# Output bias folded into the last combine, accumulator cleared by VectorE, and three items of the first expert pair kept outside the ring

## The reference

```python
gates = softmax(top_4(h @ w_router + b_router))
gu = h @ w_gu[e] + b_gu[e]                 # 1024 -> 2 x 1024
gate = minimum(gu[:, :1024], 7.0)
up = clip(gu[:, 1024:], -7.0, 7.0)
y_e = ((up + 1) * gate * sigmoid(1.702 * gate)) @ w_d[e] + b_d[e]
x = x + gt2 * sum_over_4(gates[e] * y_e)
y = rmsnorm(x, g_final)
```

## Time and profile before

| | |
|---|---|
| time, 3 runs | 1333.23, 1336.16, 1340.67 us; median 1336.16 |
| the profiled execution | 1335.32 us, its span 1333.7 us (1.6 us lie around the span) |
| mean granted TensorE clock | 0.972 of full speed |
| PE busy | 1216.4 us (91%) |
| DVE, ACT, POOL busy | 318.6, 174.3, 48.8 us |
| moved | 500.51 MB, mean 375 GB/s over the span |

### The profile page before, as it was taken

How to read it: one execution, slowest core, us unless ns; L and a number is a source line. 1 busy time by engine, 2 the same in 40 slices (tenths; PEclk the granted TensorE clock), 3 DMA queues, 4 the chain that set the end, 5 groups by cost and what they waited for, 6 DMA issues and landing times.

```text
span 1333.7 us, 15276 instructions
## 1 busy us (share of the span) xinstructions
PE 1216.4 (91%) x5982; PEld 609.9 (46%) x5982; DVE 318.6 (24%) x574; ACT 174.3 (13%) x343; POOL 48.8 (4%) x93
## 2 busy tenths in 40 slices
PE   5999998999999989898989989898989889898987
PEld 2788755688543424243242424243342424243343
DVE  2379865333212011102001110111021011102032
ACT  2132231100210200110020002001000200010012
POOL 0121231000000000000000000000000000000000
PEclk9899999999898999999999999999999999999989
DMA  9998998974499999999999999999999999999991
GB/s 352 330 357 291 381 334 335 393 296 138 190 400 414 370 415 411 413 408 417 414 419 414 421 415 421 414 420 416 417 420 413 421 411 420 415 420 416 404 409 44
DMA packets 105774, 500.51 MB, mean 375 GB/s; under 512 B 8601, under 2 KB 10759, under 8 KB 69984
## 3 DMA queue, kind: packets, MB, share of 16 engines
q1 hardware_dynamic: 98960, 478.38, 89.5%
q0 software_dynamic: 6496, 21.42, 4.6%
q10 hardware_dynamic: 272, 0.09, 0.0%
HBM read 496.48 MB, written 3.38 MB: 375 GB/s over the span
## 4 chain that ended last, share of the span: by engine, by line
PE 73%; DMA 22%; ACT 2%; DVE 1%; issue 1%; SPq 1%; DVEq 0%
PE ps L926 26%; DMA ring<-in_w_d 20%; PE ps L440 11%; PE ps L978 10%; PE ps L826 4%; PE ps L1055 4%; PE ps L876 3%; PE ps L374 3%; PE ps L803 2%; PE ps L758 2%; DMA ring<-in_w_ada 2%; PE ps L405 1%; PE ps L614 1%; ACT oT L1329 1%; PE ps L998 1%
## 5 line engine op out<-in xcount | busy, mean ns | idle before, releaser
L926 PE MATMUL ps<-ring,zone 128*64 128x512 f32 x2032 | 442.7, 592 | 2.8 <-issue 2.8
L978 PE MATMUL ps<-ring,oT 128*64 128x512 f32 x1024 | 246.5, 638 | 69.5 <-DMA ring<-in_w_d 69.5
L926 PEld LDWEIGHTS ps<-ring,zone 128*64 128x64 f32 x2032 | 147.7, 137 | 289.7 <-issue 287.2
L978 PEld LDWEIGHTS ps<-ring,oT 128*64 128x64 f32 x1024 | 77.5, 146 | 237.5 <-issue 156.6
L1877 DVE TENSOR_SCALAR zone<-ps 128x1024 f32<-128x1024 f32 x16 | 19.6, 1225 | 625.5 <-PE ps L926 625.4
L440 PE MATMUL ps<-hT,ring 128*128 128x264 f32 x640 | 152.5, 397 | 2.1 <-DVE hT L1466 1.8
L440 PEld LDWEIGHTS ps<-hT,ring 128*128 128x128 f32 x640 | 123.1, 195 | 29.6 <-issue 7.4
L1324 ACT ACTIVATE attn<-zone 128x1024 f32<-128x1024 f32 x16 | 16.9, 1057 | 502.9 <-DVE zone L1877 502.9
L826 PE MATMUL ps<-zone,dec_scores 128*64 128x512 f32 x256 | 59.3, 604 | 0.0
L1894 DVE TENSOR_TENSOR zone<-zone,ps 128x264 f32<-128x264 f32 x56 | 24.1, 430 | 145.5 <-PE ps L1055 145.5
L374 PE MATMUL ps<-ident,zone 128*128 128x128 f32 (+3 forms) x212 | 32.0, 277 | 16.5 <-DMA zone<-in_b_alpha 10.9
(11 more groups left out here) (367 smaller groups left out, 776.8 us busy)
## 6 DMA issues: line engine op xcount, KB each, us to landing
ring<-in_w_gu SPq DMA_DIRECT2D x127, 2048.0 KB, 17.6
ring<-in_w_d SPq DMA_DIRECT2D x62, 2048.0 KB, 15.6
ring<-in_w_ada SPq DMA_DIRECT2D x12, 2048.0 KB, 12.8
ring<-in_w_in SPq DMA_DIRECT2D x9, 2048.0 KB, 13.6
ring<-in_cache_k SPq DMA_DIRECT2D x32, 256.0 KB, 7.4
ring<-in_cache_k POOLq DMA_DIRECT2D x32, 256.0 KB, 6.6
ring<-in_cache_v SPq DMA_DIRECT2D x32, 256.0 KB, 9.7
ring<-in_cache_v POOLq DMA_DIRECT2D x32, 256.0 KB, 8.2
```

Of the source, the lines that this page charges most:

```text
L926: ins = pe.matmul(ps[64 * j:64 * j + CAP, c, :], xg[:, k, 2 * par + j, :], rows, start=False, stop=(k == KT - 1), skip_group_check=True)
L978: ins = pe.matmul(ps[64 * j:64 * j + CAP, 4 + c, :], hidT[:, k, j * CAP:(j + 1) * CAP], w[j][:, kk, c * 512:(c + 1) * 512], start=(k == 0) ...
```

## The change

- `SPARES = 3`: items 5, 6 and 7 of pair 0 get places outside the ring. Item 6 stays where it was. Item 7 goes to `hT` and the first 2048 columns of `zone` (2 loads, after the signal `x1_sums`). Item 5 goes to `oT`, `tok[:, 2, :]`, `rows_512` and 512 columns of `put` (4 loads, after the signal `mixed`), and to `attn` (1 load, after `pick_ready`).
- The numbers of all later items fall by 3, so that number 5, item 0 of pair 1, takes the slot of wo1 ahead of any use by PE. PE counts the three by a signal of their own, `spares_used`, on which DVE's first `swiglu` waits. PE waits once for all loads of the three (`spares_landed`), ahead of step s = 2 of the first `gate_up`. The stand-in increment of the landing semaphore is gone.
- `output_bias` is gone on PE and on DVE. DVE clears `acc` with a memset in the first quad, after it has copied the turned gates. `put` is cleared after the first `swiglu` instead of before. The product of `b_d` and gates becomes the first term of the sums of the `combine` in the last quad (`biased`). `down` of pair 0 waits for `gatesT`, and the counts of `added` and `summed` fall by 8.
- `second_half_landed` gives names of first-part signals that are used twice.

```diff
+SPARES = 3
-        spare = [[gate_hid[:, c * 512:(c + 1) * 512] for c in range(4)],
-                 [ye_tok[c // 2][:, (c % 2) * 512:(c % 2 + 1) * 512] for c in range(4)]]
+        spare = {6: [[(gate_hid, 0, 2 * FF)], [(ye_tok[0], 0, FF), (ye_tok[1], FF, FF)]],
+                 7: [[(hT_flat, 0, 2 * FF)], [(zone, 0, 2 * FF)]],
+                 5: [[(oT_flat, 0, FF), (tok[:, 2, :], FF, FF)],
+                     [(attn_flat, 0, FF), (rows_512, FF, 512), (put_512, FF + 512, 512)]]}
...
         def gate_up_done(n, first):
-            return n * 12 + (8 if first else 4)
+            return n * 12 + (8 if first else 4) - SPARES
...
             at_ = (i if edge else i - 4) if kind == "gu" else (8 + i if edge else 16 + i)
+            at_ -= 0 if kind == "gu" and edge and isinstance(n, int) and n == 0 else SPARES
...
-                    in_spare = cold and edge and s == 3
-                    if in_spare:
-                        pe.wait_ge(sig("spare_landed"), 48)
+                    in_spare = [cold and edge and 2 * s + j >= 8 - SPARES for j in range(2)]
+                    if cold and edge and s == (8 - SPARES) // 2:
+                        pe.wait_ge(sig("spares_landed"), 16 * sum(len(h) for i in range(8 - SPARES, 8) for h in spare[i]))
...
                                 if kk == 1 and c == 3:
-                                    ins.then_inc(sig("slots_used"), 1)
-                                if cold and edge and s == 0 and kk == 1 and c == 2 and j == 0:
-                                    ins.then_inc(landed[EXPERT_SLOTS[0]], 16)
+                                    ins.then_inc(sig("spares_used" if in_spare[j] else "slots_used"), 1)
...
-            def combine(q):
+            def combine(q, biased):
+                if biased:
+                    pe.wait_ge(sig("b_d"), 16)
+                    pe.wait_ge(sig("gatesT"), 1)
                 pe.wait_ge(sig("ye_ready"), q * 2 + 2)
...
+                    if biased:
+                        pe.matmul(ps[:, 6 + m % 2, 0:T], b_d_sb[:, m * P:(m + 1) * P], gatesT, start=True, stop=False)
                     for par in range(2):
                         ins = pe.matmul(ps[:, 6 + m % 2, 0:T], ye_tok[par][:, m * P:(m + 1) * P], putT[:, par, :],
-                                        start=(par == 0), stop=(par == 1))
+                                        start=(par == 0 and not biased), stop=(par == 1))
...
-                    if cold:
-                        output_bias()
...
+                if cold:
+                    pe.wait_ge(sig("gatesT"), 1)
                 down(q, 0, False, cold)
...
-                quad(q + (QUADS - 1), False, True, False)
+                quad(q + (QUADS - 1), False, True, False, biased=cold)
...
             def quad(q, qq, first, last, cold):
                 swiglu(q, 0, first)
+                if cold:
+                    chain(V.memset(put, 0.0))
...
                 if cold:
-                    output_bias()
+                    dve.wait_ge(sig("gates_turned"), 1)
+                    V.tensor_copy(gatesT, ps[0:NE, 4, 0:T]).then_inc(sig("gatesT"), 1)
+                    chain(V.memset(acc, 0.0))
...
+            def load_spare(i, kk, n):
+                home, c0, width = spare[i][kk][n]
+                k = 2 * (i // 2) + kk
+                sp.dma_start(home[:, 0:width], w_gu[0, i % 2, k * P:(k + 1) * P, c0:c0 + width])\
+                    .then_inc(sig("spares_landed"), 16)
...
+                    if phase_one and kind == "gu" and edge:
+                        if i == 2:
+                            sp.wait_ge(sig("gla_done"), 1)
+                            sp.wait_ge(sig("gla_stored"), 32)
+                            load_whole_spare(6)
+                        if i == 4:
+                            sp.wait_ge(sig("mixed"), 1)
+                            load_spare(5, 0, 0)
+                            load_spare(5, 0, 1)
+                            load_spare(5, 1, 1)
+                            load_spare(5, 1, 2)
+                        if i == 5:
+                            continue
+                        if i == 6:
+                            continue
+                        if i == 7:
+                            sp.wait_ge(sig("x1_sums"), 1)
+                            load_whole_spare(7)
+                            continue
+                    if phase_one and kind == "gu" and not edge and i == 1:
+                        sp.wait_ge(sig("pick_ready"), 1)
+                        load_spare(5, 1, 0)
```

More of the change, by code:

```diff
@@ L301, in gate_up_done @@
         def gate_up_done(n, first):
-            return n * 12 + (8 if first else 4)
+            return n * 12 + (8 if first else 4) - SPARES
         def down_done(n, last):
-            return n * 12 + (12 if last else 20)
+            return n * 12 + (12 if last else 20) - SPARES
         def expert_load(kind, i, n, edge):
             at_ = (i if edge else i - 4) if kind == "gu" else (8 + i if edge else 16 + i)
+            at_ -= 0 if kind == "gu" and edge and isinstance(n, int) and n == 0 else SPARES
             slot = EXPERT_SLOTS[at_ % SLOTS]
@@ L318, in page_of, with second_half_landed @@
             return (i, n) if item[0] == "K" else (4 * (i // 4) + n % 4, 2 * (i % 4) + n // 4)
+        def second_half_landed(item):
+            i = int(item[1:])
+            again = i >= 4 and item != "K7"
+            return sig(f"second_half_{item[0]}{i - 4 if again else i}"), 16 * (PAGES // 2) * (2 if again else 1)
         def load_pages(eng, item, half, done, slot_free):
@@ L608, in cached_values @@
                 arrived(pe, item)
-                pe.wait_ge(sig(f"second_half_{item}"), 16 * (PAGES // 2))
+                pe.wait_ge(*second_half_landed(item))
                 v = slot_ap(item)[:, 0:PAGES * WA].rearrange("p (j c) -> p j c", j=PAGES)
@@ L851, in turn_gates @@
                 ins.then_inc(sig("gates_turned"), 1)
[L853 to L862, removed]
             def gather(q, cold):
@@ L924, in gate_up @@
                             for j in range(2):
-                                rows = spare[kk][c] if w[j] is None else w[j][:, kk, c * 512:(c + 1) * 512]
+                                rows = spare_columns(2 * s + j, kk, c) if in_spare[j] else w[j][:, kk, c * 512:(c + 1) * 512]
                                 ins = pe.matmul(ps[64 * j:64 * j + CAP, c, :], xg[:, k, 2 * par + j, :], rows,
@@ L938, in turn_hidden @@
                         pe.wait_ge(sig("read"), q * 10 + (3 + 2 * par + g))
-                    if par == 1:
-                        pe.wait_ge(sig("added"), q * KT + (7 + g))
+                    if par == 1 and not cold:
+                        pe.wait_ge(sig("added"), q * KT + (g - 1))
                     for k in range(4):
@@ L1071, in quad @@
                     turn_hidden(q, 0, cold, first)
-                    combine(q - 1)
+                    combine(q - 1, biased)
                     gate_up(q, 1, False, False)
+                if cold:
+                    pe.wait_ge(sig("gatesT"), 1)
                 down(q, 0, False, cold)
-                turn_hidden(q, 1, cold, first and not cold)
+                turn_hidden(q, 1, cold, first)
                 turn_put(q)
@@ L1875, in swiglu @@
                 n = q * 2 + par
+                if isinstance(n, int) and n == 0:
+                    dve.wait_ge(sig("spares_used"), SPARES)
                 dve.wait_ge(sig("slots_used"), gate_up_done(n, first))
@@ L1992, in rounds_and_gates @@
                 dve.wait_ge(sig("gates"), 1)
[L1994 to L2001, removed]
             one_round(0)
@@ L2088, in _, with load_whole_spare @@
             dn = w_d[0].rearrange("e (k p) c -> e p k c", p=P)
[L2090 to L2095, removed]
+            def load_spare(i, kk, n):
[3 more added lines that the diff above has]
+                    .then_inc(sig("spares_landed"), 16)
+            def load_whole_spare(i):
+                for kk in range(2):
+                    for n in range(len(spare[i][kk])):
+                        load_spare(i, kk, n)
             def load_expert(kind, n, pair, edge, phase_one=False, rows=None):
@@ L2182, in second_half @@
             def second_half(item):
-                load_pages(pool, item, 1, sig(f"second_half_{item}"), freed[slot_before(item)])
+                load_pages(pool, item, 1, second_half_landed(item)[0], freed[slot_before(item)])
             arrived(pool, "ka")
```

32 lines of the change are left out of this document (17 added, 15 removed).

## The result

Slower: 1341.64 us against 1333.25 (medians of 20 runs each), a ratio of 1.0054 with a 95% interval of 1.0033 to 1.0075, or 7.2 us. The ratio is of the fast runs alone, which leaves out one run of the changed kernel (1353.38 us); the medians are of all. I had forecast 1.9 us less, and 1327 to 1339. The profiled execution has a span of 1344.3 us, 10.6 above the one of before.

A forecast was written before the change was run, and what follows sets the result against it. The expert part was taken as bound by bytes, with the DMA queue empty at times because the ring is full. -5.5 + 3.6 = -1.9 us took 1335.32 to 1333.4, or 1334.2 for a median; range 1327 to 1339.

The forecast's parts named there:

- the gain of 5.5 us: Second quad: old item 26 begins at 457.3 instead of 462.8, 5.5 us earlier, which includes the head's 1.9.
- Outside items: First lull: two more items fill empty time; queue full 362 to 387, empty until 396, 1.9 us left of 10.1.
- Rival A: Head: the head start is kept whole, -10.1 + 3.6 = -6.5 us, 1329.7; chance 0.10.
- D: First gate_up: the single wait for three outside items holds PE; clearly slower, +0.5% needs landing past 375; chance 0.06.
- Bias out of the first quad: First quad: without output_bias, down ends at 435.7 instead of 441.1 and the next gate_up begins at 448.3 instead of 453.7.
- A lead kept to the end: Loops after the second quad: the 5.5 us gain enters the final sum unchanged, with no term for loss.
- Bias in the last combine: Last quad: 16 bias records at 0.23 us each, say 3.6 us, all on PE's path, moving the end by 3.6.
- The upper bound, 5.4: Last combine: the bias costs at most 5.4 us, if its products ran as in output_bias.
- The sum: Whole kernel: -5.5 + 3.6 = -1.9 us, 1335.32 becomes 1333.4, 1334.2 for a median.
- Rival B: Last quad: the bias is hidden, the dip at 1248 being not the ring; -5.5 us, 1330.7; chance 0.13.
- C: Second quad: PE not early, gap at 458 stays, 1.9 won against 3.6 paid; +1.7 us, 1337.9; chance 0.09.
- first-byte figure: SP loads: first byte at some 0.6 us, in place of 1.9, would make the gain about 6.8 instead of 5.5.

The follow-up runs named there:

- e11: Changed kernel with only items 6 and 7 outside the ring, item 5 back in it, and the bias in the first quad; ratio to the kernel before 1.0006.
- e3: Changed kernel with b_d and the turned gates padded by zero rows to 128 for the bias products; ratio to the kernel before 1.0012.
- e2: Kernel before with the bias part alone: bias products in the last combine, acc cleared by memset, one item outside; ratio to the kernel before 1.0044.
- e4: Changed kernel with the bias products left out altogether, so the output lacks the share of b_d; ratio to the kernel before 0.9990.
- e5: Changed kernel with the eight 32-row bias products in each of the seven combines instead of the last alone; ratio to the kernel before 1.0353.
- e6: Changed kernel with bias products padded to 128 rows in each of the seven combines; ratio to the kernel before 1.0162.
- e1: Changed kernel with the bias put back in the first quad, ahead of down, three items still outside; ratio to the kernel before 0.9978.
- e7: Changed kernel with the bias in the first quad, between the two halves of the first down; ratio to the kernel before 0.9981.
- e12: Repeat measurement of the changed kernel with the bias put back in the first quad, three items outside; ratio to the kernel before 0.9989.
- e9: Changed kernel with products of no use, five ahead of the first half of each down and three ahead of the second; ratio to before 1.0087.
- e10: Changed kernel with bias in the first quad and products of no use, two ahead of each down's first half, one ahead of second; ratio to before 1.0047.

## Why the prediction was wrong

Two steps of the sum failed: the gain of 5.5 us, of which 2.8 were there at 520 in the traced execution and nothing at 600, and the 3.6 us for the bias in the last combine, which made that combine 6.4 longer and cost 6.1 in the lead.

**Outside items: right.** Issues at 303 to 305, 340 and 349, the queue full to 387 and empty to 397, step 2 of the first `gate_up` without a wait. Rival A fell as said, and e11 shows it from the other side. D did not happen. The memsets of VectorE took 1.82 and 0.70 us and delayed nothing.

**Bias out of the first quad: the place right, the size off.** I had `gate_up` of the second quad at 448.3; it began at 450.9. The second half of the first `down` started at 429.50 (I had 428.6) and took 8.8 us instead of 7.1, behind a wait of 4.49; the granted clock from 429 to 434 was 0.66:

```profile
417.93 7.09 PE L984 MATMUL ps<-ring,oT 128*64 128x512 f32 x32 [1.07 <-DMA ring<-in_w_d]
429.50 8.78 PE L984 MATMUL ps<-ring,oT 128*64 128x512 f32 x32 [4.49 <-DMA ring<-in_w_d]
...
450.89 27.64 PE L934 MATMUL ps<-ring,zone 128*64 128x512 f32 x128
481.03 8.78 PE L984 MATMUL ps<-ring,oT 128*64 128x512 f32 x32 [2.50 <-DMA ring<-in_w_d]
492.79 9.99 PE L984 MATMUL ps<-ring,oT 128*64 128x512 f32 x32 [2.98 <-DMA ring<-in_w_d]
```

So 2.8 us were won by 520 instead of 5.5. I had taken PE's work at its full clock and left out that the products behind a wait can go at half of it.

**A lead kept to the end: false.** My sum carries the 5.5 us from the second quad to the end unchanged; for what the loops between may lose it has no term, and I gave no reason. In the changed kernel all of the lead was lost by 590. Near 492 the second half took 10.0 us instead of 7.1 (the last row above), the next use that frees a slot came that much later, and the queue ran dry at 523; again 8.7 at 557 and the dip at 585. In that half the granted clock was 0.50 (the lower level, 1.2 GHz) from 493 to 498, and 1.00 again from 500 on:

```profile
493.00:496.00 3.00, 3.00 (x8) 0.90 (x8) 0.00 (x0) 0.00 (x0) 0.00 (x0) 0.50 1.01 421
500.00:503.00 3.00, 3.00 (x17) 1.07 (x14) 0.00 (x0) 0.16 (x1) 0.00 (x0) 1.00 1.01 421
```

The place of the bias makes it likely, but not certain. Of the executions without filling, those with the bias out of the first quad (the changed kernel, e2, e3, e4, e5, e6) had second halves of 10.0, 9.7, 8.6, 8.5, 10.1 and 7.1 us there, behind waits of 3.0, 4.3, 2.7, 2.6, 2.8 and 2.5; those with it in (before, e1, e7, e11, e12) 7.1, behind 1.8, 0.4, 0.2, 0.3 and 1.4. The first four lost 4.6, 3.7, 1.1 and 1.1 us from 520 to 600. e5 lost 9.4 and e6 3.4, with one biased combine in that stretch, which costs 6.1 and 3.3; so about 3.3 and nothing are left for the halves. Those with the bias in lost nothing. e4 is the changed kernel up to the last quad, so between 1.1 and 4.6 lies the chance of an execution, and what settles it is open. The times are the better measure: the ratio of e4 (1.3 us ahead of before) says that of the 5.5 us forecast some 4 were not there. e9, with PE kept busy, lost 0.4.

The same step is found far behind the first quad too, with the bias in:

```profile
1031.39 9.94 PE L997 MATMUL ps<-ring,oT 128*64 128x512 f32 x32 [3.14 <-DMA ring<-in_w_d]
1060.00:1064.00 4.00, 4.00 (x21) 1.30 (x18) 0.00 (x0) 0.00 (x0) 0.00 (x0) 1.00 0.52 129
```

These are a second half of e12 and the stretch 29 us on, where 2.5 us of its lead went. e2 had two more, of 10.05 and 10.06 us at 1042.8 and 1165.7, and lost 2.7 and 2.4 us behind them.

**Bias in the last combine: mis-sized.** "16 records: 3.7 us, say 3.6" should have been 6.4. That it would be wholly on the path was right (6.1 us by the lead). I priced a record by the mean of a combine in which all are of one height, and took from L861 that fewer rows are no quicker; neither row can show what a neighbour of another height costs. At one height it would have come out: 10.9 us in e3 against 7.36 are 3.5. The upper bound, 5.4, had the same hole.

**The sum.** With what was measured: -2.8 + 4.6 + 6.1 = +7.9 us, and +2.7 more in the profiled execution. Those 2.7 are open: all second halves of that stretch took 7.1. e1 and e12 are the same kernel, and their steps from 600 to 1240 are +0.6 and +3.9, of which 2.5 follow the one long half above; the rest seems to be chance of an execution. By the times of many runs the account is: 1.3 us won without the bias (e4), 8.5 us lost by the bias (the changed kernel against e4), in sum 7.2 slower, where I had 5.5 won and 3.6 lost; each of the two carries some 3 or 4 us of uncertainty. By the ratio the change costs 7.2 us.

Rival B was wrong: nothing of the bias was hidden at the end. C is nearest to the outcome, a lead that is not there when the bias has to be paid, but not by its own sign: the second quad's `gate_up` came at 450.9 and not later than 452, and the lead was lost afterwards.

By the first-byte figure of the Trainium skill (DMA: Bandwidth & Descriptors, Specifications) the second quad's `gate_up` would, by my estimate, have come 1.3 us ahead of my 448.3, and it was 2.6 behind. That does not test the figure by itself, for PE's slow half is in it. The slow start of the trace stands: issued at 395.26, the loads moved 207 GB/s from 395 to 399, so full rate counts from 397.0, 1.75 us behind the issue.

## What to carry to other kernels

In a loop that is bound by bytes through a ring, ask for each place whether PE's next use is what lets the next load go. If so, every microsecond of PE's is paid there, and the same work can be nearly free elsewhere, where PE waits for data: in e1 the 5.8 us of bias made the second quad's `gate_up` 1.1 us later than in the changed kernel, at the same lead at 400. The best of the versions tried leave the bias in the first quad and keep the outside items, at 0.998 and 0.999 (e1 and e12, one kernel) and 0.998 (e7).

Price a product with its neighbours: in this combine a few of another height among tall ones made all of them slower, and padding with zero rows was cheaper. And a wait of PE's can cost more than itself, by the slower products behind it, in one execution and not in the next: read more than one trace before you put a number on it.

## What the runs showed of the hardware that I had not expected

- Products over 32 rows between products over 128 rows: 0.64, 0.55 and 0.54 us a step against 0.45 for all of one height; no weight load ahead across the change (0.34 us of pause in the loads).
- A 128 x 512 float32 product with 128 columns of weights took 0.90 us (in e9, 10 records in 4.5), where one with 64 columns, alternating between the two halves of the outputs, takes 0.43 (32 records, 16 products, in 6.9).
- Second halves of `down` of 7.1, 8.5 to 8.8, or 9.7 to 10.1 us for the same 32 records. The length of the wait ahead does not settle which: waits of 3.1 us were mostly followed by 7.1, but three times by 9.9 to 10.1 (e12, and e2 twice), one of 2.6 by 8.5 (e4), and in e10 14 waits of 2.1 us five times by 7.1 and nine times by 8.8.
